# Column sums and first gates of an adaptive-norm modulation as float32r products of a rounded part and a rest

## The reference, cut to what matters

```
def adaln_pre_norm(x, c, g, w_mod, b_mod):
    mod = jax.nn.silu(c) @ w_mod + b_mod           # c: (1, 1024), w_mod: (1024, 3072)
    shift, scale, gate = jnp.split(mod, 3, axis=-1)
    h = rms_norm_2(x, g, NORM_EPS) * (1.0 + scale[:, None, :]) + shift[:, None, :]
    return h, gate
for i in range(DEPTH):                             # DEPTH = 2: l = 0 before the convolution, l = 1 before the dilated attention
    h, gate = adaln_pre_norm(x, c, norm_g[i], w_mod[i], b_mod[i])
    y = mixer(h)
    x = x + gate[:, None, :] * y
```

## Time and profile before

| what | value |
|---|---|
| median of 3 runs | 1069.6 us (1061.01, 1069.6, 1069.96) |
| span of the profiled execution, first to last instruction | 1066.7 us |
| TensorE busy | 1048.1 us, 98% of the span |
| VectorE busy | 771.7 us, 72% |
| ScalarE busy | 590.3 us, 55% |
| GpSimd busy | 120.4 us, 11% |

### The profile page before, as it was taken

One profiled execution on the slowest core, in us unless ns is written; L12 is line 12 of the kernel. 1 busy time (PEld: TensorE's weight loads), 2 busy tenths in 40 slices (PEclk: granted clock), 3 DMA queues, 4 the chain that ended last, 5 costly groups with the idle time before them and its releaser, 6 DMA issues.

```text
span 1066.7 us, 25458 instructions
## 1 busy us (share of the span) xinstructions
PE 1048.1 (98%) x10480; PEld 996.2 (93%) x10485; DVE 771.7 (72%) x1090; ACT 590.3 (55%) x900; POOL 120.4 (11%) x131
## 2 busy tenths in 40 slices
PE   9999999999999999999999999999999999999997
PEld 8966999999999899997899999999998999999985
DVE  5987666766789689768766676786676877775586
ACT  6586555555456783334555454564544667666452
POOL 0230010100000028841000000000000000000000
PEclk9999999999999999999999999999999999999999
DMA  8734687888634510002678777737653656556401
GB/s 308 251 90 137 216 286 266 271 296 280 204 122 155 163 61 5 3 11 74 217 250 287 255 252 264 276 121 228 197 192 112 212 181 199 171 195 196 143 2 59
DMA packets 83073, 192.23 MB, mean 180 GB/s; under 512 B 6000, under 2 KB 6912, under 8 KB 82992
## 3 DMA queue, kind: packets, MB, share of 16 engines
q1 hardware_dynamic: 74256, 159.93, 45.3%
q0 software_dynamic: 7584, 27.53, 7.8%
q10 hardware_dynamic: 1152, 3.59, 1.0%
HBM read 189.45 MB, written 1.05 MB: 179 GB/s over the span
## 4 chain that ended last, share of the span: by engine, by line
PE 88%; DVE 6%; issue 2%; ACT 2%; DMA 2%; POOL 0%; DVEq 0%; POOLq 0%; ACTq 0%
PE bank L2308 13%; PE bank L2310 13%; PE bank L2309 13%; PE bank L2659 5%; PE bank L2658 5%; PE bank L2660 5%; PE bank L2325 4%; PE bank L2345 4%; PE bank L2877 4%; PE bank L2275 2%; PE bank L2276 2%; PE bank L2277 2%; PE bank L2263 1%; PE bank L2265 1%; PE bank L2264 1%
## 5 line engine op out<-in xcount | busy, mean ns | idle before, releaser
L1350 DVE TENSOR_TENSOR w_lo<-raw,w_hi 128x1024 fp32r<-128x1024 f32 x295 | 357.8, 1223 | 199.2 <-ACT w_hi L737 198.7
L737 ACT ACTIVATE w_hi<-raw 128x1024 fp32r<-128x1024 f32 x295 | 310.3, 1059 | 291.4 <-PE bank L2310 150.4
L2308 PE MATMUL bank<-act_hi,w_hi 128*128 128x256 f32 x1200 | 334.0, 278 | 0.4 <-DVE w_lo L1350 0.3
L2309 PE MATMUL bank<-act_lo,w_hi 128*128 128x256 f32 x1200 | 332.9, 277 | 0.0
L2310 PE MATMUL bank<-act_hi,w_lo 128*128 128x256 f32 x1200 | 332.8, 277 | 0.0
L2308 PEld LDWEIGHTS bank<-act_hi,w_hi 128*128 128x128 f32 x1200 | 225.3, 188 | 1.7 <-DVE w_lo L1350 0.9
L2310 PEld LDWEIGHTS bank<-act_hi,w_lo 128*128 128x128 f32 x1200 | 225.3, 188 | 0.0
L2309 PEld LDWEIGHTS bank<-act_lo,w_hi 128*128 128x128 f32 x1200 | 225.0, 187 | 0.0
L2658 PE MATMUL bank<-w_hi,ff_hi 128*128 128x256 f32 x512 | 141.5, 276 | 0.0
L2659 PE MATMUL bank<-w_lo,ff_hi 128*128 128x256 f32 x512 | 141.5, 276 | 0.0
L2660 PE MATMUL bank<-w_hi,ff_lo 128*128 128x256 f32 x512 | 141.5, 276 | 0.0
(11 more groups left out here) (375 smaller groups left out, 1675.4 us busy)
## 6 DMA issues: line engine op xcount, KB each, us to landing
raw<-in_mlp_w_up_dram SPq DMA_DIRECT2D x64, 512.0 KB, 3.7
raw<-in_mlp_w_down_dram SPq DMA_DIRECT2D x64, 512.0 KB, 6.1
raw<-in_dil_w_in_dram SPq DMA_DIRECT2D x64, 512.0 KB, 4.1
mod_w<-in_w_mod_dram POOLq DMA_DIRECT2D x48, 512.0 KB, 5.9
raw<-in_conv_w_in_dram SPq DMA_DIRECT2D x32, 512.0 KB, 4.5
raw<-in_rwkv_w_rkv_dram SPq DMA_DIRECT2D x24, 512.0 KB, 4.1
raw<-in_dsa_w_in_dram SPq DMA_DIRECT2D x12, 512.0 KB, 8.1
raw<-in_dsa_w_o_dram SPq DMA_DIRECT2D x8, 512.0 KB, 4.5
```

The source lines that it names most:

```text
L737: act.activation(w_hi[:, slot, :], raw[:, slot, :], ACT.Copy).then_inc(hi_ready, 1)
L1350: dve.tensor_tensor(w_lo[:, slot, :], raw[:, slot, :], w_hi[:, slot, :].bitcast(F32), ALU.subtract).then_inc(lo_ready, 1)
L2308: pe.matmul(dst, w_hi[:, slot, at], hi[:, kt, :], start=begin, stop=False, skip_group_check=True)
L2309: pe.matmul(dst, w_hi[:, slot, at], lo[:, kt, :], start=False, stop=False, skip_group_check=True)
```

## The change

Both sums over partitions are made from a rounded part and a rest, in float32r. While ScalarE is idle at the end of each MLP it copies ones into `ones_r` and rounds `mod_all[n]` into `MOD_HI[n]` (the free slots of the MLP's activations, and `mod_w[2]` for the gate); VectorE takes the rest in place (`MOD_LO[n]`). That needs `mod_all` a step earlier, so rows are weighed one step ahead: step 0 weighs rows 0 and 1, step k row k + 1, the last step none. The columns become two accumulating products each with two columns of ones; the gates of l = 0 two each; the gates of l = 1 stay as they were. Both parts of the columns of l = 0 now stand between the tiles, because the mix overwrites the place where the rounded part lies.

```
+    def mod_split_plan(t):
+        ones_r = t("ones_r", [P, P], F32R)
+        t("mod_hi_under", [P, 4 * BLOCK + 2 * D - P])
+        return dict(ones=ones_r, hi=t("mod_hi", [P, D], F32R), lo=t("mod_lo", [P, 3 * D], F32R))
+    MOD_SPLIT = (3, 2)
 # ScalarE, end of mlp(l)
+    act.wait_ge(up_sq, done + 2 * FF_STEPS)
+    act.activation(ONES_R, ones, ACT.Copy).then_inc(mod_hi_ready, 1)
+    act.wait_ge(granule_used, base + 8 * last + PER_BLOCK)
+    for n in range(MOD_SPLIT[l]):
+        act.wait_ge(mod_used[n], KT * (l + 1))
+        act.activation(MOD_HI[n], M["mod_all"][:, n * D:(n + 1) * D], ACT.Copy).then_inc(mod_hi_ready, 1)
 # VectorE, mlp(l)
         if q == 2 and not isinstance(it, int):
-            weigh_mod(l, 2, it)
+            weigh_mod(l, 2, it, 1)
     split_lo(base, 8, it)
     rest_mid(it, 0)
+    if isinstance(it, int):
+        for n in range(3):
+            weigh_mod(l, n, 0)
     for q in range(1, PER_BLOCK):
         split_lo(base, 8 + q, it)
-    weigh_mod(l, 0, it)
-    weigh_mod(l, 1, it)
+    for n in range(2):
+        weigh_mod(l, n, 1 if isinstance(it, int) else it, 0 if isinstance(it, int) else 1)
...
-    weigh_mod(l, 2, 0)
+    weigh_mod(l, 2, 1)
...
-    for n in range(2 if l else 3):
-        weigh_mod(l, n, last)
+    for n in range(MOD_SPLIT[l]):
+        dve.wait_ge(mod_hi_ready, (MOD_SPLIT[0] + 1) * l + n + 2)
+        dve.tensor_tensor(MOD_LO[n], M["mod_all"][:, n * D:(n + 1) * D], MOD_HI[n].bitcast(F32), ALU.subtract).then_inc(mod_lo_ready, 1)
 # VectorE, conv()
-    weigh_mod(1, 2, KT - 1)
 # TensorE
-    for k in range(KT * part, KT * (part + 1)):
-        mm = pe.matmul(bank[(1, 3)[l]][:, k:k + 1], M["mod_all"][:, k * P:(k + 1) * P], ones[:, 0:1], start=True, stop=True)
+    two = ONES_R[:, 0:2]
+    for k in range(KT):
+        to, at = bank[(1, 3)[l]][:, 2 * (KT * part + k):2 * (KT * part + k + 1)], slice(k * P, (k + 1) * P)
+        pe.matmul(to, MOD_HI[part][:, at], two, start=True, stop=False)
+        mm = pe.matmul(to, MOD_LO[part][:, at], two, start=False, stop=True)
+def mod_gate_split(n, banks):
+    at = slice(n * BLOCK, (n + 1) * BLOCK)
+    if n == 0:
+        pe.wait_ge(mod_lo_ready, 3)
+    pe.matmul(bank[banks[n]][:, :], ONES_R, MOD_HI[2][:, at], start=True, stop=False)
+    pe.matmul(bank[banks[n]][:, :], ONES_R, MOD_LO[2][:, at], start=False, stop=True).then_inc(mod_full, 1)
 # TensorE, rwkv_in()
-    turn_scaled(1, X, RKV_TURN, lambda: mod_columns(0, 0))
-    mod_columns(0, 1)
-    mod_gate(0, (4, 5))
-    mod_gate(1, (4, 5))
+    def columns_between():
+        mod_columns(0, 0)
+        mod_columns(0, 1)
+    turn_scaled(1, X, RKV_TURN, columns_between)
+    mod_gate_split(0, (4, 5))
+    mod_gate_split(1, (4, 5))
```

More of the change, by code:

```diff
@@ L315, in program @@
         M = scope(mlp_plan)
+        MR = scope(mod_split_plan)
         R = scope(rwkv_plan)
@@ L318, in program @@
         less = mixer["vT"]
+        MOD_HI = (M["hi"][:, 0, :, :].rearrange("p k t -> p (k t)"), M["lo"][:, 0, :, :].rearrange("p k t -> p (k t)"),
+                  MR["hi"][:, :])
+        MOD_LO = tuple(MR["lo"][:, n * D:(n + 1) * D] for n in range(3))
+        MOD_SPLIT = (3, 2)
+        ONES_R = MR["ones"][:, :]
         C = scope(conv_plan)
@@ L364, in program @@
         mod_full, mod_ready = sem("mod_full"), sem("mod_ready")
+        mod_hi_ready, mod_lo_ready = sem("modulation_sums_hi_ready"), sem("modulation_sums_lo_ready")
         up_relu, up_sq, mid_hi, mid_lo = sem("up_relu"), sem("up_sq"), sem("mid_hi"), sem("mid_lo")
@@ L1652, in dsa, with weigh_mod @@
                 take_out("dsa_out", "mlp0")
-            def weigh_mod(l, n, k):
+            def weigh_mod(l, n, k, ahead=0):
                 part, total = M["mod_w"][:, n, :], M["mod_all"][:, n * D:(n + 1) * D]
@@ L1659, in weigh_mod @@
                 else:
-                    dve.wait_ge(mod_loaded[n], k * 16 + 16 * (KT * l + 1))
+                    dve.wait_ge(mod_loaded[n], k * 16 + 16 * (KT * l + 1 + ahead))
                 if isinstance(k, int) and k == 0:
@@ L1663, in weigh_mod @@
                 else:
-                    dve.wait_ge(mod_used[n], k + KT * l)
-                    c = c_col[:, k:k + 1] if isinstance(k, int) else c_col[:, bass.ds(k, 1)]
+                    dve.wait_ge(mod_used[n], k + (KT * l + ahead))
+                    c = c_col[:, k:k + 1] if isinstance(k, int) else c_col[:, ahead:KT][:, bass.ds(k, 1)]
                     dve.scalar_tensor_tensor(total, part, c, total, ALU.mult, ALU.add).then_inc(mod_used[n], 1)
@@ L1748, in modulation @@
                 dve.wait_ge(mod_full, 4 * l + 2)
-                dve.tensor_tensor(mod_col[:, l, :], bank[(1, 3)[l]][:, 0:2 * KT], B_MOD[l], ALU.add).then_inc(mod_ready, 1)
+                dve.tensor_tensor(mod_col[:, l, :], bank[(1, 3)[l]][:, 0:4 * KT:2], B_MOD[l], ALU.add).then_inc(mod_ready, 1)
             def mod_gain(l):
@@ L2716, in mod_columns @@
                 if part == 0:
-                    for n in range(2 if l else 3):
-                        pe.wait_ge(mod_used[n], KT * (l + 1))
+                    pe.wait_ge(mod_lo_ready, MOD_SPLIT[0] * l + 2)
                     if l:
```

## The result

The changed kernel took 1078.4 us, the median of four runs (1072.03, 1078.35, 1078.48, 1081.56), against 1065.3 us for the kernel before in the same series (four runs, 1060.81 to 1069.96). The ratio is 1.0116, with a 95% interval of 1.0073 to 1.0158. The forecast was 1071.4 us with a range of 1062 to 1076: in this series the change slows the kernel by about 13 us where I had worked out 2, and the time lies outside the range. In a second series the unaltered changed kernel took 1077.04 us (12 runs, 1063.21 to 1083.32) against 1066.67 (23 runs), 10 us more, ratio 1.0062, 1.0027 to 1.0097. (Every ratio leaves out runs more than 1.5% above the fastest of their kernel, which here are the longest of the changed kernel's; that is why this ratio is smaller than that of the medians.)

A forecast was written before the change was run, and what follows sets the result against it. The prediction took TensorE, busy 98% of the span, as the bound, fed by a ScalarE and VectorE chain at the RWKV entry. That entry's +1.8 us, all other terms 0, on the median 1069.6 gave 1071.4 us, range 1062 to 1076.

The forecast's parts named there:

- The products at the RWKV entry, the load: RWKV entry column sums: a float32r load costs 112 ns as before, 3.58 us before and after, so no gain.
- the second rival: Float32r loads cost only 56 ns: `turned` not later, convolution starts 1.05 us earlier, 1068.6 us; chance 0.10.
- The gates: RWKV entry: four float32r products 0.235 us apart save 0.74 us, swallowed by a TensorE wait of about 1.3 us.
- The move: RWKV entry: both column halves ahead of tile 1's turn make `turned` 1.79 us later; sum there +1.8 us.
- The convolution's entry: Start of the convolution: column loads at equal price, TensorE not waiting for VectorE; cost 0, otherwise up to 1.1 us.
- The end of the MLPs: ScalarE's new copies fit its idle time, VectorE's subtractions replace weighings; cost 0, or 0.3 us without cover.
- Step 0 of both MLPs: VectorE waits for row 1, but granule 12's split has 1.7 to 2 us of cover; taken 0, range 0 to 1.2.
- Rival 4: Step 0: row 1's loads land late and slow the kernel; at 10 us 4 us more, 1075.4; chance 0.05.
- Something larger than the sum: Long float32r stretches run at 112.8 or 117.5 ns a matmul; the dilated attention's pace is worth 5.4 us.
- Rival 1: The convolution is entered at the slower pace, the stream ahead now being float32r: 3.6 us more, 1075.0; chance 0.17.
- Rival 3: A faster dilated attention, 5.4 us less: 1066.0 us, down to 1062.8; chance 0.15.
- The sum: Whole kernel: +1.8 us, profiled span 1066.7 to 1068.5, median 1069.6 to 1071.4 us; chance 0.50.

The follow-up runs named there:

- between_only: The kernel before with only the move: both float32 halves of the columns between the turns of the two tiles; 1067.17 us against 1067.52, ratio 1.0015.
- early_row0: The changed kernel with row 0 weighed ahead of the split of granule 8 in step 0, so row 1's loads start earlier; 1068.94 us, ratio 1.0012 to the kernel before.
- wide32: The changed kernel with row 0 weighed earlier and 32 columns of ones in place of 2; 1069.44 us against 1065.51 for the kernel before, ratio 1.0027.
- both_fixes: The changed kernel with row 0 weighed earlier and the second half of the columns behind tile 1's turn again; 1066.23 us, ratio 1.0001 to the kernel before.
- rows_only: The kernel before with only the rows weighed a step ahead, sums still float32 and in their old place; 1075.89 us against 1067.52, ratio 1.0112.
- old_columns: The changed kernel with the second half of the columns of l = 0 behind tile 1's turn again; 1074.30 us, ratio 1.0081 to the kernel before.
- after_again: The changed kernel once more, unaltered, for a second profiled execution; 1077.04 us (12 runs) against 1066.67 for the kernel before, ratio 1.0062.
- wait_each: The kernel before with six dummy VectorE reductions at the end of each of steps 0 to 6 of MLP 0; 1107.28 us, ratio 1.0379.
- dve_wait: The kernel before with dummy VectorE reductions at the end of step 0, 5 in MLP 0 and 7 in MLP 1; 1084.26 us, ratio 1.0179.
- wait_mlp0: The kernel before with five dummy VectorE reductions at the end of step 0 of MLP 0 alone; 1068.69 us against 1068.63, ratio 1.0014.
- split_only: The changed kernel with rows weighed in their own step again, the last row ahead of the MLP's last three splits; 1078.66 us, ratio 1.0100 to the kernel before.

## Why the prediction was wrong

- **The products at the RWKV entry, the load.** Right. 32 float32r loads took 3.64 us, 0.11 us each. The Trainium skill, "TensorE: Matmul & The Clock Gate", section "Weight-path perf modes", has the fast weight load on for 128 weights of a type that is not FP32; by these rows float32r doesn't get it (0.19 us recorded a load, as for float32, against 98 ns for bf16), and the second rival (cheap loads, 1068.6) falls with it. The gates came out 0.22 to 0.24 us apart (0.32 at the first, as the clock came back), and TensorE waited 1.28 us behind them, as said; the releaser that the profile names is `mod_col` on VectorE, not ScalarE's rounding.
- **The move.** The mechanism and the size were right: between_only gives +1.79. What I didn't have is the fall of the granted clock behind 32 narrow float32r products in one piece. It brings the term to +2.41 in the changed kernel, +2.11 in its second execution, +2.78 and +3.06 in the two variants where it lasted for 6.8 us. Mis-sized by 0.3 to 1.3 us.
- **The convolution's entry.** Right: 0.0 up to the first granule and behind it in early_row0, wide32 and both_fixes, which all have the new columns. The +3.4 us of the changed kernel are the pace, below.
- **The end of the MLPs.** Right: 0.
- **Step 0 of both MLPs.** This step failed, in both of its numbers. "Taken: 0" rested on the median of 5.9 us of the loads, but blocks of row 1 were there only 7.4 and about 9 us after their issue, in the profiled execution of the changed kernel. Of the four traces of kernels with this order (the changed kernel twice, rows_only, old_columns) the cover of 1.7 to 2 us was used up in MLP 0 in one and in MLP 1, for which no rows had been read, in all four. I had read the bound of 8.4 us as a cost of 0.6 us. And its price was wrong in kind: I priced a wait at its length. Its length was 0.25 to 0.5 us. What follows it is up to 4.8 us in MLP 0, 4.9 in MLP 1 and 3.4 in the convolution. Rival 4 named the mechanism's place and asked for loads of 12.5 us to be slower by over 1%; with loads of 9 us the first series gives 1.0116.
- **Something larger than the sum.** I had the fact that decides: two paces, "taken up where a stretch is entered and kept until a wait". I used it for the stages whose entry the change touches (rivals 1 and 3) and did not put it together with the one wait that the change adds. Both sides of that sentence stood in the prediction, some paragraphs apart. Rival 1, the convolution at the slower pace, came true with its price (+3.42 against 3.6), for another reason than given: the convolution took the pace of MLP 1, not that of the new column sums (both_fixes has these and is fast; rows_only has not and is slow). Rival 3 came true in the profiled execution (-5.0 in the dilated attention, with -1.8 behind it), and that is luck, not the change: after_again has it slow.
- **The sum.** Of the 9.9 us between the two profiled spans: +0.9 are waits at step 1, +9.7 the pace in the MLPs, +3.4 the pace in the convolution, +2.4 the RWKV entry, -6.8 the dilated attention and what follows it, +0.4 the start and the rest of the RWKV layer. My sum held 1.8 of it.

With the pace priced, the sum is: 2.1 to 2.4 us at the RWKV entry, 0.4 + 4.9 + 3.4 = 8.7 us by a wait in MLP 1, and 5.3 us more where MLP 0 waits as well. On the 1066.7 us of the last series' kernel before that gives 1077.5 to 1077.8 us with the wait in MLP 1 alone and about 1083 with both; the median there was 1077.04, the longest run 1083.32. The sum is made after the fact, and leaves out the dilated and the last attention, which are 1.7 to 6.8 us shorter in some executions.

## What to carry to other kernels

Where an engine's stream is near its limit, look first whether the same instructions run at more than one pace in different stretches; if so, an added wait can cost the whole stretch behind it, and not its own length alone. Cover of 1 to 2 us over the median of a DMA is no cover, since loads of 512 KB landed here between 3.8 and 9.1 us after their issue in one trace. Moving three weighings ahead of one split and one rest, by which the loads are issued some 4 us earlier, won back all that this change had lost in the MLPs. And where products are paced by their weight loads, one float32 product (two recorded loads) costs the same as the two float32r products that take its place, so splitting these column sums gained nothing.

## What the runs showed of the hardware

- **Two paces of 256-column float32r products**, 113.3 and 117.8 ns, at a granted clock of 1.00 and with the same instructions. The kernel before shows them side by side in its first MLP: the up products of step 0, and then the rest. TensorE by window in the kernel before:

```profile
117.00:141.00 24.00, 24.00 (x206) 1.00 0.72 248
143.00:290.00 147.00, 147.00 (x1296) 1.00 0.81 276
```

  A pace begins behind a wait or where one kind of product gives way to another, and the throw is not fixed by the program (wait_each: three of five steps slow; dve_wait against wait_mlp0). Over all traces, MLP 0 of wait_each apart: of the 19 MLPs without a wait at step 1 all 19 entered it at the fast pace, of the 8 with one 7 at the slow pace to their end, and one (wait_mlp0) for half a step. The convolution ran at MLP 1's pace in all 14 traces, slow in five of them. What it physically is stays open: DMA share and rate are the same, 0.79 and 266 GB/s, in the slow MLP 0 of the changed kernel and in the fast one of rows_only, which speaks against contention with transfers. No run shows a way to hold the fast pace behind a wait.
- **The granted clock fell behind 32 weight-bound float32r products in one piece**, with no gap over 0.11 us in TensorE's records: in every trace that has them so (the changed kernel twice, early_row0, wide32, split_only), for 3.4 or 6.8 us. It began 2.7 to 3.8 us after the first of them, in early_row0 and wide32 before the last had started. It is in none with 16 and 16 (old_columns, both_fixes) or with 32 recorded float32 products in their place (between_only, one trace). The Trainium skill, "TensorE: Matmul & The Clock Gate", section "HAM oscillation — how this bites in real kernels", puts such falls down to idle gaps of TensorE between its bursts. The falls behind the long waits of dve_wait, wait_each and split_only agree with it; this one, without a gap, does not.
- **The landing of the same three loads** differed by 2 us between two executions of one kernel (5.5 and 7.4 us for the first), with the same program around them.
